# Layer 1 of the first block: memory heads between differential heads, gate panels last, the gates' sigmoid from exponential and logarithm

## The reference, cut to what matters

```python
k_sh, v_sh = jnp.split(rms_norm(x, kv_norm) @ w_kv, 2, axis=-1)       # 6 + 6 panels of 128
q, gate, q_mem, g_mem = jnp.split(rms_norm(x, pre_norm) @ b_w_in, ...) # 6 + 6 + 2 + 2 panels
lam = exp(sum(lq1 * lk1)) - exp(sum(lq2 * lk2)) + lam_init
p = softmax(q k^T + bias)                        # 6 heads, 2 score maps each
o = rms_norm((p[0] - lam * p[1]) @ v, subln) * (1 - lam_init)
y_mem = softmax(q_mem k_mem^T / 8) @ v_mem       # 4 heads of 64
y = concat(o * silu(gate), y_mem * silu(g_mem)) @ w_out
x = x + rms_norm(y, post_norm)
```

## Time and profile before

| | us |
|---|---|
| median of 3 runs | 1397.03 (1394.84 to 1401.82) |
| profiled execution | 1397.52 |
| its span | 1395.7 |
| mean granted TensorE clock | 0.955 |
| PE busy in the span | 1281.3 (92%) |
| DVE, ACT, POOL busy | 858.1, 626.5, 165.1 |
| chain that ended last | PE 72%, DVE 14%, ACT 9%, issue 4% |

### The profile page before, as it was taken

How to read it: one execution, slowest core, us unless ns; L and a number is a source line. 1 busy time by engine, 2 the same in 40 slices (tenths; PEclk the granted TensorE clock), 3 DMA queues, 4 the chain that set the end, 5 groups by cost and what they waited for, 6 DMA issues and landing times.

```text
span 1395.7 us, 23837 instructions
## 1 busy us (share of the span) xinstructions
PE 1281.3 (92%) x9682; PEld 1218.8 (87%) x9682; DVE 858.1 (61%) x1492; ACT 626.5 (45%) x1078; POOL 165.1 (12%) x166
## 2 busy tenths in 40 slices
PE   6988689977799689999998999889999998999997
PEld 6977678857789489999998999878999998999997
DVE  5667845235667457666547774657845656776642
ACT  5765322144345455444433344454345544644431
POOL 3127200000000101221002200001300000122100
PEclk9999899798999699999999999989999999999999
DMA  7433200012344137555534543324554444655561
GB/s 246 143 121 107 93 14 16 16 42 95 106 140 140 38 131 257 181 169 165 166 110 132 177 161 107 100 76 152 180 166 161 143 136 152 215 193 182 157 200 37
DMA packets 53597, 185.78 MB, mean 133 GB/s; under 512 B 6768, under 2 KB 8944, under 8 KB 53232
## 3 DMA queue, kind: packets, MB, share of 16 engines
q1 hardware_dynamic: 53056, 181.23, 40.2%
q10 hardware_dynamic: 432, 3.03, 0.6%
HBM read 183.19 MB, written 1.05 MB: 132 GB/s over the span
## 4 chain that ended last, share of the span: by engine, by line
PE 72%; DVE 14%; ACT 9%; issue 4%; DMA 1%; POOL 1%; DVEq 0%; ACTq 0%; POOLq 0%
PE bank L2317 19%; PE bank L2320 19%; PE bank L2318 19%; DVE wl L1790 3%; ACT wh L1440 3%; PE bank L2329 2%; PE bank L2420 1%; PE bank L2302 1%; PE bank L2375 1%; DVE zl L1882 1%; PE bank L2388 1%; DVE sqr L1886 1%; PE bank L2338 1%; ACT scb L1671 1%; PE bank L2437 1%
## 5 line engine op out<-in xcount | busy, mean ns | idle before, releaser
L2317 PE MATMUL bank<-xh,wh 128*128 128x256 f32 (+1 forms) x2008 | 590.2, 294 | 22.2 <-DVE xl L2024 10.2
L2320 PE MATMUL bank<-xh,wl 128*128 128x256 f32 (+1 forms) x2008 | 578.1, 288 | 4.2 <-DVE wl L1790 4.2
L2318 PE MATMUL bank<-xl,wh 128*128 128x256 f32 (+1 forms) x2008 | 579.2, 288 | 0.0
L1790 DVE TENSOR_TENSOR wl<-raw,wh 128x1024 fp32r<-128x1024 f32 (+1 forms) x343 | 423.5, 1239 | 228.6 <-ACT wh L1440 226.9
L1440 ACT ACTIVATE wh<-raw 128x1024 fp32r<-128x1024 f32 (+1 forms) x343 | 356.0, 1043 | 307.8 <-PE bank L2320 293.7
L2317 PEld LDWEIGHTS bank<-xh,wh 128*128 128x128 f32 x2008 | 387.9, 193 | 32.3 <-issue 21.9
L2320 PEld LDWEIGHTS bank<-xh,wl 128*128 128x128 f32 x2008 | 389.0, 194 | 5.0 <-DVE wl L1790 5.0
L2318 PEld LDWEIGHTS bank<-xl,wh 128*128 128x128 f32 x2008 | 388.4, 193 | 1.0
L1391 POOL TENSOR_TENSOR hl<-tmp,hh 128x272 fp32r<-128x272 f32 (+1 forms) x44 | 53.2, 1210 | 458.1 <-ACT hh L1704 458.1
L2317 PE MATMUL bank<-hh,wh 128*128 128x272 f32 (+1 forms) x352 | 100.3, 285 | 0.0
L2318 PE MATMUL bank<-hl,wh 128*128 128x272 f32 (+1 forms) x352 | 100.2, 285 | 0.0
(11 more groups left out here) (351 smaller groups left out, 1606.8 us busy)
## 6 DMA issues: line engine op xcount, KB each, us to landing
raw<-w_ffn_gate SPq DMA_DIRECT2D x44, 512.0 KB, 3.5
raw<-w_ffn_up SPq DMA_DIRECT2D x44, 512.0 KB, 3.6
raw<-w_a_w_in SPq DMA_DIRECT2D x29, 512.0 KB, 3.5
raw<-w_ffn_down SPq DMA_DIRECT2D x32, 448.0 KB, 3.4
raw<-w_w_out SPq DMA_DIRECT2D x16, 512.0 KB, 3.5
raw<-w_b_w_in SPq DMA_DIRECT2D x16, 512.0 KB, 4.1
raw<-w_ffn_down SPq DMA_DIRECT2D x16, 512.0 KB, 3.5
raw<-w_ret SPq DMA_DIRECT2D x16, 512.0 KB, 3.6
```

The lines of the kernel that those rows point to most:

```text
L1790: v.tensor_tensor(lo[:, c], raws[n % N_RAW][:, c], hi[:, c].bitcast(F32), ALU.subtract).then_inc(*w_lo.up(n))
L2317: pe.matmul(ps, hi[:, c], x_hi(k), start=(k == 0), stop=False)
L2318: pe.matmul(ps, hi[:, c], x_lo(k), start=False, stop=False)
L2320: last = pe.matmul(ps, lo[:, c], x_hi(k), start=False, stop=(k == kt - 1))
```

## The change

Five things:

1. The streams are mixed: differential heads 0 and 1, memory head 0, differential 2, memory 1, differential 3, memory 2, differential 4, memory 3, differential 5. `skewed` calls `fill` before every second live stream, and the `fill()` calls inside the streams are fewer.
2. The panels' order changes: query panel 1 directly behind query panel 0 and ahead of the first key panel; the memory queries' and memory gates' panels early; the six gate panels 6 to 11 held back and put into `between` only when head 5's first step is reached.
3. Each gate's sigmoid is made where its panel leaves PSUM, from one table set: DVE takes the maximum with -80, ACT does exp(-x), log(1 + that) and exp of its negative, POOL multiplies as before. A fifth `tmp` buffer joins the ring.
4. In layer 1 gating and splitting of y go by pairs of tiles (128x512), with the memory pair split first. The output projections of both layers take their eight k tiles in the order 6, 7, 0 to 5, so the memory pair first. Layer 0's splitting (`branch0`, DVE L1993, ACT L1612 and L1615) keeps its order, the memory pair last.
5. Lambda's steps move to the start of the program, between panels of the memory keys and values of layer 0.
The number of panels and of matmuls in them is the same.

```diff
-LAYER1_BETWEEN = [pair for h in range(1, BT) for pair in (("b_w_in", h), ("w_kv", h), ("w_kv", BT + h - 1))] \
-    + [("w_kv", 2 * BT - 1)] + [("b_w_in", p) for p in list(range(12, 16)) + list(range(6, 12))]
+LAYER1_BETWEEN = [("w_kv", 1), ("w_kv", 6), ("b_w_in", 12), ("b_w_in", 14), ("b_w_in", 2), ("w_kv", 2), ("w_kv", 7),
+                  ("b_w_in", 13), ("b_w_in", 15)]
+LAYER1_BETWEEN += [pair for h in range(3, BT) for pair in (("b_w_in", h), ("w_kv", h), ("w_kv", BT + h - 1))]
+LAYER1_BETWEEN += [("w_kv", 2 * BT - 1)] + [("b_w_in", p) for p in range(6, 12)]
...
     order += [("w_out0", p, KT) for p in range(KT)]
-    order += [("b_w_in", 0, KT), ("w_kv", 0, KT)]
+    order += [("b_w_in", 0, KT), ("b_w_in", 1, KT), ("w_kv", 0, KT)]
...
-def skewed(streams):
+def skewed(streams, between=None):
...
             live.append(streams.pop(0))
-        for g in list(live):
+        for n, g in enumerate(list(live)):
+            if between and n % 2:
+                between()
...
         ysq1 = sb("sq", [P, KT, S], ph)
+        tmp1.append(sb("tmp4", [P, S], ph))
...
             do("x_norm")
+            b, freed = bank.take()
+            do("lam", b, freed)
+            bank.give(b, (lam_e, 0))
...
+            do("lam_use")
...
-            q_evac, k_evac, g_evac = scaled("q", 0), scaled("k", 0), scaled("gate", 6)
-            qm_evac, gm_evac = scaled("qm", 12), scaled("gm", 14)
+            def gate_of(which, first_panel):
+                def evac(panel, b, n):
+                    i = panel - first_panel
+                    do("proj1", which, i, b, n)
+                    t, f_t = tmp.take()
+                    do("silu1", which, i, t, f_t)
+                    tmp.give(t, (sil1, (which, i)))
+                    return ((ev1, (which, i)),)
+                return evac
+            q_evac, k_evac, qm_evac = scaled("q", 0), scaled("k", 0), scaled("qm", 12)
+            g_evac, gm_evac = gate_of("gate", 6), gate_of("gm", 14)
+            tmp.give(4)
...
             do("kv_split")
+            project("b_w_in", [1], "pre1", S, q_evac, keep=True)
...
-            b, freed = bank.take()
-            do("lam", b, freed)
-            bank.give(b, (lam_e, 0))
-            between.extend(LAYER1_BETWEEN)
+            between.extend(LAYER1_BETWEEN[:-6])
...
                 need("w_kv", h)
+                if h == BT - 1:
+                    between.extend(LAYER1_BETWEEN[-6:])
...
                 stb_ring.give(st, (d_p, h))
-                fill()
+                fill(2 if h == 0 else 1)
...
                 scb_ring.give(pb, (d_tr, h))
-                fill()
+                if h == 0:
+                    fill()
...
                 ptb_ring.give(pt, (d_o, h))
-                fill()
...
                 tmp.give(r, (d_r, h))
-                fill()
...
                 g = memory_head(1, h)
-                for _ in range(2):
-                    next(g)
-                    fill()
-                    yield
-                if h == 0:
-                    need("b_w_in", 11)
-                    for which, n in (("gm", MT), ("gate", BT)):
-                        for i in range(n):
-                            t, f_t = tmp.take()
-                            do("silu1", which, i, t, f_t)
-                            tmp.give(t, (sil1, (which, i)))
+                next(g)
+                yield
+                next(g)
+                need("b_w_in", 14 + h // 2)
+                yield
...
-            skewed([diff_head(h) for h in range(BT)] + [memory_stream(h) for h in range(MEM_HEADS)])
-            do("branch")
+            skewed([diff_head(0), diff_head(1), memory_stream(0), diff_head(2), memory_stream(1), diff_head(3),
+                    memory_stream(2), diff_head(4), memory_stream(3), diff_head(5)], fill)
+            while between:
+                fill()
+            settle()
+            for j in range(3):
+                do("branch", j)
+            for j in (3, 0, 1, 2):
+                do("y1_split", j)
...
                     s.activation(xh[:, BT:KT, 0:S], qm0[:, :, :], ACT.Copy, scale=1.0).then_inc(*in_hi.up(("y0", 3)))
-                elif kind == "branch":
-                    for i in range(BT):
-                        on.wait_ge(*branch.past(i))
-                        s.activation(xh[:, i, 0:S], rh1[:, i, :], ACT.Copy, scale=1.0).then_inc(*in_hi.up(("y1", i)))
-                    for j in range(MT):
-                        on.wait_ge(*ym.past((1, 2 * j + 1)))
-                        s.activation(xh[:, BT + j, 0:S], qm1[:, j, :], ACT.Copy, scale=1.0).then_inc(
-                            *in_hi.up(("y1", BT + j)))
+                elif kind == "y1_split":
+                    j, = a
+                    on.wait_ge(*used.past(STREAM.index(("b_w_in", 11, 0, KT))))
+                    on.wait_ge(*(ym.past((1, MEM_HEADS - 1)) if j == 3 else branch.past(j)))
+                    s.activation(xh[:, 2 * j:2 * j + 2, 0:S], qm1[:, :, :] if j == 3 else pair(rh1, j), ACT.Copy,
+                                 scale=1.0).then_inc(*in_hi.up(("y1", j)))
...
                 elif kind == "silu1":
...
-                    buf = gm1 if which == "gm" else gate1
-                    on.wait_ge(*ev1.past((which, i)))
-                    after(on, f_t)
-                    sigmoid(tmp1[t][:, :], buf[:, i, :], ("1" + which, i))
+                    x, key = tmp1[t][:, :], (which, i)
+                    tables(ACT.Exp)
+                    on.wait_ge(*sg_c.past(key))
+                    s.activation(x, x, ACT.Exp, scale=-1.0).then_inc(*sg_e.up(key))
+                    on.wait_ge(*sg_e.past(key))
+                    s.activation(x, x, ACT.Ln, bias=one).then_inc(*sg_l.up(key))
+                    on.wait_ge(*sg_l.past(key))
+                    s.activation(x, x, ACT.Exp, scale=-1.0).then_inc(*sg.up(("1" + which, i)))
...
                 elif kind == "branch":
-                    for i in range(BT):
+                    j, = a
+                    for i in (2 * j, 2 * j + 1):
...
                         on.wait_ge(*sil1.past(("gate", i)))
-                        v.tensor_tensor(rh1[:, i, :], rh1[:, i, :], gate1[:, i, :], ALU.mult).then_inc(*branch.up(i))
-                    for i in range(KT):
-                        src = rh1[:, i, :] if i < BT else qm1[:, i - BT, :]
-                        on.wait_ge(*in_hi.past(("y1", i)))
-                        v.tensor_tensor(xl[:, i, 0:S], src, xh[:, i, 0:S].bitcast(F32), ALU.subtract).then_inc(
-                            *in_lo.up(("y1", i)))
+                    v.tensor_tensor(pair(rh1, j), pair(rh1, j), pair(gate1, j), ALU.mult).then_inc(*branch.up(j))
+                elif kind == "y1_split":
+                    j, = a
+                    c = slice(2 * j, 2 * j + 2)
+                    on.wait_ge(*in_hi.past(("y1", j)))
+                    v.tensor_tensor(xl[:, c, 0:S], qm1[:, :, :] if j == 3 else pair(rh1, j),
+                                    xh[:, c, 0:S].bitcast(F32), ALU.subtract).then_inc(*in_lo.up(("y1", j)))
...
                                            ALU.mult).then_inc(*ev1.up((which, i)))
+                elif kind == "silu1":
+                    which, i, t, f_t = a
+                    buf = gm1 if which == "gm" else gate1
+                    on.wait_ge(*ev1.past((which, i)))
+                    after(on, f_t)
+                    v.tensor_scalar(tmp1[t][:, :], buf[:, i, :], -80.0, None, ALU.max).then_inc(*sg_c.up((which, i)))
...
                                     ALU.mult).then_inc(*lam_a.up(0))
+                elif kind == "lam_use":
...
                     after(on, freed)
-                    for k in range(k0, k0 + nk):
+                    order = [KT - 2, KT - 1, *range(KT - 2)] if tag in ("y0", "y1") else list(range(k0, k0 + nk))
+                    for k in order:
...
-                        on.wait_ge(*ready.past((tag, k // 2 if tag == "y0" else k)))
-                        pe.matmul(ps, hi[:, c], x_hi(k), start=(k == 0), stop=False)
+                        on.wait_ge(*ready.past((tag, k // 2 if tag in ("y0", "y1") else k)))
+                        pe.matmul(ps, hi[:, c], x_hi(k), start=(k0 == 0 and k == order[0]), stop=False)
...
                         on.wait_ge(*w_lo.past(n))
-                        last = pe.matmul(ps, lo[:, c], x_hi(k), start=False, stop=(k == kt - 1))
+                        last = pe.matmul(ps, lo[:, c], x_hi(k), start=False,
+                                         stop=(k0 + nk == kt and k == order[-1]))
```

9 lines of the change are left out of this document (6 added, 3 removed).

## The result

The changed kernel takes 1412.4 us in the median of 4 runs (1408.3 to 1413.7), the kernel before 1398.4 us beside it. The ratio of their times is 1.0091 (95% interval 1.007 to 1.0113): slower, by some 13 us. The forecast was 1402.1 us, so it had the direction of the sum right and its size wrong by 10 us. The profiled execution of the changed kernel took 1408.32 us (span 1406.5), 10.8 us more than that of before (1397.52). It is the fastest of the four; the other three ran at a mean granted clock of 0.947 or 0.948 against 0.954 in the profiled one, and have no trace. So 10.8 us can be followed here, and 3 to 4 us of the median cannot.

What follows compares the result with a forecast made beforehand. Layer 1's tail was taken as bound by dependent steps of single memory heads. Terms -4.2 + 0.3 - 1.4 - 15.8 + 15.9 + 3.0 + 5.5 + 1.8 = +5.1 us gave a 1402.1 us median, 8-in-10 range 1390 to 1410.

Steps and rivals of the forecast that it cites:

- layer 0's wait for the memory pair: Layer 0's output projection starts later because the memory pair is still split last on DVE: +1.8 us (1.5 to 2).
- old tail goes: Layer 1's 26.2 us after the last input projection disappear, while their 10.3 us of matmuls are done elsewhere: -15.8 us.
- stretch without projections: Between last value panel and first gate panel, four gaps and a half-pace first gate panel: +15.9 us (9 to 20).
- head 5's end: Behind the second gate panel, last value product and norm wait for copied values behind one gate's sigmoid: +3.0 us (1 to 4).
- pace of the last four gate panels: Layer 1's gate panels after head 5's norm: forecast at 2.9 us each, with no added term.
- last gate panel to output projection: End of layer 1: last gates' scaling, activations, POOL product, gating and splitting before the output projection: +5.5 us (4.5 to 6.5).
- front and small waits: Layer 1's front -4.2 us, lambda's work in the start phase +0.3, small waits between heads -1.4.
- slower rival: Head 5's gap or light work keeps the clock low, remaining gate panels at half pace: 1409 us with three panels; chance 0.20.
- The gates' activation: Three activations per gate plus DVE and POOL work hide behind each 2.9 us gate panel, except the last; part of +5.5 us.

Runs made afterwards that it cites:

- e1: The changed kernel with layer 0's output projection back in the order 0 to 7 of its input tiles: 1408.2 us, 1.0076 of the kernel before.
- e4: The changed kernel with the activations of gates 0 and 1 given out behind head 5's norm: 1406.5 us, 1.0062 of the kernel before.
- e6: The changed kernel with layer 0's memory pair split ahead of the group norms, other pairs each behind its norm: 1403.9 us, 1.0035 of the kernel before.
- e5: The changed kernel with the gates' activation back as one table sigmoid, without VectorE's bound: 1404.5 us, 1.0038 of the kernel before.
- e9: The kernel before with only the sigmoid changed to bound, exponential, logarithm, exponential, all eight in one go at their old place: 1404.7 us, ratio 1.0041.
- e2: The changed kernel with all six gate panels in the list between heads from the start, none held back: 1394.4 us, 0.9975 of the kernel before.

## Why the prediction was wrong

By its own terms, from the profiled executions. Between the statistics of layer 1 and its output projection the changed kernel needs 149.5 us (343.00 to 492.52) against 140.2 (340.89 to 481.13), +9.3, where the terms gave +3.0.

| step | predicted us | measured us |
|---|---|---|
| layer 0's wait for the memory pair | +1.8 | +1.8 (6.11 - 4.30; e1) |
| old tail goes | -15.8 | -15.8, taken over |
| stretch without projections | +15.9 | +17.4 (25.5 - 9.7, and 1.6 in the first gate panel) |
| head 5's end | +3.0 | +5.4 (462.35 to 469.93, less 2.2) |
| pace of the last four gate panels | 0 | +2.4 |
| last gate panel to output projection | +5.5 | +8.3 |
| front and small waits | -5.6 | -8.4, by difference |

The output projection's first three panels then take 9.9 us against 10.9, since the level was back sooner; with it the distance is 10.0 us longer.

Right were the mechanisms of layer 0, of the front (no wait for the split keys, 2.94 us for head 0's scaled keys against 3.0), and of the stretch. There the time was near but its parts were not, so that the sum came out is partly luck. The first three waits came to 7.2 us and not to 9.2 (1.8, 2.2 and 5.2), and the matmuls lost 7 us to the level. It fell to 0.50 at 434 us, after a wait of 1.59 us among short operations, was full again from 440.7 to 444.1 and then at 0.50 until 457.8. I had it fall only at the wait of 5 us, because the kernel before kept its level through the 2.03 us ahead of 347.56.

Wrong were two steps. **Head 5's end** counted one gate's three activations ahead of the copied values. The rows show two, since VectorE scales the first gate only at 463.66, behind the low halves of two weights and head 4's scaled output; e4 takes them away and 3.81 us become 0.73. Behind that longer wait the level was at half from 468.0 to 474.9, in most of the next gate panel, the 2.4 us of the fifth row. The slower rival had named this with the same cause, and in e4, without the wait, the level stays full. Its size is partly chance: in e1 and e6, with the same code there and waits of 3.73 and 3.58 us, the level was at half for 3.4 us only, and the time from head 5's norm to the end of the last gate panel is 12.9 and 13.3 us instead of 14.3.
**The gates' activation** failed in one sentence: "Per gate panel of 2.9 us ACT does a high half and 1.3 us, DVE 1.2 + 0.8, so they hide, except the last." Each engine's sum is under 2.9 us, but they wait for each other in turn, and the ring takes 4.3 us. So at the end two gates were due and not one: 8.3 us. e5 shortens the ring and the wait with it, to 5.68. I had also priced the three steps by busy time and not by what stands behind them on ScalarE, which in the kernel before costs 4 to 6 us (e9).

The front and the small waits came 2.8 us better than I said, by difference. The waits of over 0.4 us from the statistics to the last value panel fell from 10.5 us to 5.3, which is near the 5.6 forecast. The other 3 us are not placed: the old tail's 15.8 us were taken over and not measured anew. The level doesn't explain them. It was at 0.50 around head 0's scores for longer in this trace than in e2's, whose code is the same there and which is 2.2 us quicker.

Of the causes, the held-back panels weigh most: without them (e2) the distance is 16.3 us shorter and the kernel is faster than before. The forecast knew the stretch and its cost, but took it as a price of the change; it was a choice of its own, which paid nothing. The 3 to 4 us between the profiled run and the median stay open. Traces of the same code differ by 2 to 3 us through the level, and the three other runs had a lower mean clock, so the level may be their cause; this is not shown.

## What to carry over

Work that can fill waits should be spread as widely as the waits are; held back for the last ones it leaves others bare, and its own activations come due when nothing is left to cover them. Two in-order engines that hand work back and forth are as slow as the ring through both, so add up the ring and not each engine's share. Splits and scalings of parts that are ready early belong ahead of the last part's chain. And where two traces differ by 2 or 3 us, look for the place before naming a cause: stretches of the same code differed by as much here.
